# Products by halves around two norms, the first heads' groups turned beside the last items, half-width sums of squares added up by GpSimd

## The reference, cut to what matters

```python
def trunk_layer(x, mod, lw, lam, l_init, ffn, ctx):
    shift1, scale1, gate1, shift2, scale2, gate2 = jnp.split(mod, 6, axis=-1)
    h = rmsnorm(x, lw['norm_mix']) * (1 + scale1) + shift1
    y, state = token_mixer(h, lw, lam, l_init, ctx)      # 6 differential heads | convolution | 6 latent heads, then @ w_out
    x = x + gate1 * y
    h = rmsnorm(x, lw['norm_ffn']) * (1 + scale2) + shift2
    x = x + gate2 * ffn(h)                               # layer 0: dense SwiGLU; layer 1: top 2 of 8 experts
    return x, state

def rmsnorm(x, g):
    xf = x.astype(F32)
    y = xf * lax.rsqrt(jnp.mean(xf * xf, axis=-1, keepdims=True) + EPS)
    return (y * g.astype(F32)).astype(x.dtype)
```

## Time and profile before

| what | value |
|---|---|
| time, median of 3 runs | 2053.76 us (2052.38 to 2057.56) |
| span of the profiled execution | 2053.3 us; the page gives no other time for it |
| PE busy | 1881.8 us, 92% |
| DVE busy | 1393.7 us, 68% |
| ACT busy | 1022.6 us, 50% |
| POOL busy | 311.6 us, 15% |
| PE's share of the chain that ended last | 77% |

### The profile page before, as it was taken

One profiled execution on the slowest core, in us unless ns is written; L12 is line 12 of the kernel. 1 busy time (PEld: TensorE's weight loads), 2 busy tenths in 40 slices (PEclk: granted clock), 3 DMA queues, 4 the chain that ended last, 5 costly groups with the idle time before them and its releaser, 6 DMA issues.

```text
span 2053.3 us, 28528 instructions
## 1 busy us (share of the span) xinstructions
PE 1881.8 (92%) x11244; PEld 1701.7 (83%) x11244; DVE 1393.7 (68%) x1956; ACT 1022.6 (50%) x1371; POOL 311.6 (15%) x491
## 2 busy tenths in 40 slices
PE   5999789897999999997998789897999999999994
PEld 3987678697999999997988678696788888888883
DVE  5375885535666567555474885535898988898987
ACT  4235686623221211213135686623777777777772
POOL 0082540000000000000073541010000000000002
PEclk8999799998999999998999799997999999999998
DMA  9225300022454444422122000014999999999996
GB/s 330 63 92 194 99 1 1 21 89 96 134 164 155 134 159 144 139 83 67 53 68 71 1 1 1 1 23 156 399 391 405 404 407 389 404 399 395 375 396 230
DMA packets 112438, 366.22 MB, mean 178 GB/s; under 512 B 7456, under 2 KB 65216, under 8 KB 85936
## 3 DMA queue, kind: packets, MB, share of 16 engines
q1 hardware_dynamic: 94448, 303.50, 39.3%
q0 software_dynamic: 13536, 48.39, 7.1%
q10 hardware_dynamic: 4320, 12.49, 1.5%
HBM read 349.23 MB, written 15.12 MB: 177 GB/s over the span
## 4 chain that ended last, share of the span: by engine, by line
PE 77%; DVE 11%; ACT 5%; DMA 3%; issue 3%; POOL 1%; SPq 0%; DVEq 0%; POOLq 0%; ACTq 0%
PE PS L2108 33%; PE PS L2049 25%; PE PS L2088 5%; PE PS L1777 5%; PE PS L1893 4%; PE PS L1865 3%; ACT E L844 2%; DVE NM L1217 1%; ACT PT L849 1%; DVE KCn L1177 1%; DMA araw<-in_w_ada_head 1%; DVE E L1228 1%; DVE SS L1160 1%; DVE split L1497 1%; DMA raw<-in_w_ada_head 1%
## 5 line engine op out<-in xcount | busy, mean ns | idle before, releaser
L2108 PE MATMUL PS<-H,split 128*128 128x320 f32 x2688 | 402.9, 312 | 8.8 <-DVE H L1697 7.2
L2108 PEld LDWEIGHTS PS<-H,split 128*128 128x128 f32 x2688 | 400.8, 191 | 11.9 <-issue 10.8
L1019 ACT CAST split<-raw 128x2048 fp32r<-128x2048 f32 (+2 forms) x64 | 112.8, 1763 | 284.3 <-PE PS L2108 242.1
L1497 DVE TENSOR_TENSOR split<-raw,split 128x2048 fp32r<-128x2048 f32 (+2 forms) x64 | 138.0, 2161 | 126.5 <-ACT split L1019 126.5
L1412 DVE TENSOR_TENSOR msplit<-raw,msplit 128x2048 fp32r<-128x2048 f32 x82 | 187.9, 2292 | 37.0 <-ACT msplit L976 37.0
L2049 PE MATMUL PS<-split,HT 128*128 128x512 f32 x816 | 197.0, 397 | 2.8 <-DVE HT L1391 2.4
L1412 DVE TENSOR_TENSOR split<-raw,split 128x2048 fp32r<-128x2048 f32 x82 | 186.8, 2289 | 18.3 <-ACT split L976 18.3
L976 ACT CAST msplit<-raw 128x2048 fp32r<-128x2048 f32 x82 | 157.0, 1915 | 70.4 <-PE PS L2049 61.6
L2049 PE MATMUL PS<-msplit,HT 128*128 128x512 f32 x816 | 191.0, 389 | 0.7 <-DVE msplit L1412 0.7
L1777 PE MATMUL PS<-split,H 128*128 128x384 f32 (+1 forms) x960 | 171.1, 340 | 12.8 <-DVE split L1497 9.5
L2049 PEld LDWEIGHTS PS<-split,HT 128*128 128x128 f32 x816 | 152.8, 191 | 34.5 <-DVE HT L1391 2.8
(11 more groups left out here) (326 smaller groups left out, 2827.1 us busy)
## 6 DMA issues: line engine op xcount, KB each, us to landing
raw<-in_moe_w_gate SPq DMA_DIRECT2D x55, 1024.0 KB, 7.5
raw<-in_moe_w_down SPq DMA_DIRECT2D x55, 1024.0 KB, 7.9
raw<-in_moe_w_up SPq DMA_DIRECT2D x54, 1024.0 KB, 7.3
DOTW<-in_w_ada_rows POOLq DMA_DIRECT2D x56, 512.0 KB, 3.9
raw<-in_w_ada_head SPq DMA_DIRECT2D x16, 1024.0 KB, 7.1
mraw<-in_moe_w_up SPq DMA_DIRECT2D x14, 1024.0 KB, 7.2
mraw<-in_moe_w_gate SPq DMA_DIRECT2D x13, 1024.0 KB, 7.3
mraw<-in_moe_w_down SPq DMA_DIRECT2D x13, 1024.0 KB, 7.8
```

Source lines behind the costliest of these rows:

```text
L1019: A.copy(split[u % 2][:, 0, 0:w], src[:, 0:w]).then_inc(S["split_hi"], 1)
L1497: V.tensor_tensor(split[u % 2][:, 1, 0:w], src[:, 0:w], split[u % 2][:, 0, 0:w].bitcast(f32), ALU.subtract).then_inc(S["split_lo"], 1)
L2108: ins = T.matmul(PS[:, 4 * (u % 2) + 2 * c + hf, 0:HALF], W[:, w, k, c * P:(c + 1) * P], A[:, a, k, hf * HALF:(hf + 1) * HALF], start=(k = ...
```

## The change

Four things. (1) The two units before and the two units after norms 1 and 2 run as *pairs* by halves of 320 tokens: first half of both units, then second half of both. The norm runs on the first half of the tokens while PE does the second half of the pair ahead of it, and on the second half while PE does the first half of the pair behind it. The reciprocal root is copied from PSUM to `RSTD` in SBUF by ACT, and sums and roots are taken for three groups of columns per half. (2) For chunks 4 to 7 the squares are 320 wide, in `SQH`, and GpSimd adds them to `XACC`. (3) The five `QA` groups are turned in iterations 53 to 57, through bank 1, and the convolution's high part is rounded in iteration 58; after the last item only the `OC` groups are left, and the first output unit starts on the `QA` chunks when four of them are turned, the fifth being turned behind its first chunk. (4) PE's loop over the FFN rounds is written out. Buffers are moved (`H`, `MIX`, `QA`, `KA`, `VA`, `VC`, `KCn`, `ACTB`) so that the halves don't overwrite what is still read.

```diff
+K_MIX = ITEMS - NT - 2
@@ GpSimd
+            def add_half_squares(q):
+                first = SQUARES[q] + 4
+                for i in range(8):
+                    hf = i // 4
+                    pool.wait_ge(S["sq_ready"], first + i + 1)
+                    pool.wait_ge(S["sq_used"], first + i)
+                    acc = XACC[:, hf * HALF:(hf + 1) * HALF]
+                    nc.gpsimd.tensor_tensor(acc, acc, SQH[:, i % 2, :], ALU.add).then_inc(S["sq_used"], 1)
@@ ScalarE, norm_halves (ua is the first unit of the pair ahead of the norm)
+                half_square(0, 4)
+                half_square(0, 5)
+                A.activation(XWARM[:, :], eps[:, :], ACT.Sqrt)
+                half_square(0, 6)
+                half_square(0, 7)
+                half_root(0)
+                rstd_copy(0)
+                split_hi(ua + 2)
+                shifted_hi(0)
+                half_square(1, 4)
+                half_square(1, 5)
+                shifted_hi(1)
+                shifted_hi(2)
+                half_square(1, 6)
+                half_square(1, 7)
+                split_hi(ua + 3)
+                for i in range(3, 7):
+                    shifted_hi(i)
+                half_root(1)
+                shifted_hi(7)
+                rstd_copy(1)
+                for i in range(KC, 2 * KC):
+                    shifted_hi(i)
@@ VectorE, norm_halves
+                half_add(0, 0)
+                half_add(1, 0)
+                x_mean(q, 0)
+                x_rstd(q, 0)
+                half_add(0, 1)
+                scaled(0)
+                scaled(1)
+                split_lo(ua + 2)
+                shifted_lo(0)
+                scaled(2)
+                shifted_lo(1)
+                half_add(1, 1)
+                scaled(3)
+                shifted_lo(2)
+                for i in range(4, 7):
+                    scaled(i)
+                    shifted_lo(i - 1)
+                x_mean(q, 1)
+                scaled(7)
+                shifted_lo(6)
+                x_rstd(q, 1)
+                shifted_lo(7)
+                split_lo(ua + 3)
+                scaled(8)
+                for i in range(9, 2 * KC):
+                    scaled(i)
+                    shifted_lo(i - 1)
+                shifted_lo(2 * KC - 1)
@@ TensorE
             for k in range(-2, ITEMS + 1):
+                if 0 <= k - K_MIX < NT:
+                    t = k - K_MIX
+                    if t == 0:
+                        pe.wait_ge(S["turn_out"], (l + 1) * TURNS)
+                    else:
+                        pe.wait_ge(S["mix_lo"], l * 10 + t)
+                    pe.wait_ge(S["subln_gained"], l * NT + t + 1)
+                    mix_turn(t, 1, QA[:, t, :])
                 if k + 2 < ITEMS:
...
-            for w in range(2 * NT):
...
-            pe.wait_ge(S["mix_lo"], (l + 1) * 10)
-            pe.wait_ge(S["conv_lo"], l + 1)
+            for i in range(4):
+                mix_turn(NT + i, 4 + i, OC[:, TILE_ORDER[i], :])
+            def mixed(k):
+                if k == 0:
+                    pe.wait_ge(S["mix_lo"], l * 10 + NT)
+                if k == 1:
+                    pe.wait_ge(S["mix_lo"], l * 10 + NT + 1)
+                    mix_turn(2 * NT - 1, 4, OC[:, TILE_ORDER[4], :])
+                if k == MIX_CONV[0]:
+                    pe.wait_ge(S["conv_lo"], l + 1)
+                if k == MIX_C[0]:
+                    pe.wait_ge(S["mix_lo"], (l + 1) * 10)
+            def first_half_sums(hf, i, k):
+                if (hf, i, k) == (1, 0, 4):
+                    x_sum_half(1, 0)
+                if (hf, i, k) == (1, 1, 0):
+                    x_rows_half(1, 0)
...
+            def pair(u, k_chunks, A, ready=None, free=None, halves=False):
+                for hf in range(2):
+                    for i in range(2):
+                        v = u + i
+                        if hf == 0:
+                            free(v)
+                            pe.wait_ge(S["split_lo"], v + 1)
+                        W = split[v % 2][:, :, 0:k_chunks * 256].rearrange("p s (k n) -> p s k n", k=k_chunks)
+                        for k in range(k_chunks):
+                            if ready is not None:
+                                ready(hf, i, k)
+                            for c in range(2):
+                                for w, a in ((0, 0), (0, 1), (1, 0)):
+                                    ins = T.matmul(PS[:, 4 * (v % 2) + 2 * c + hf, 0:HALF], W[:, w, k, c * P:(c + 1) * P],
+                                                   A(a, k, hf),
+                                                   start=(k == 0 and w == 0 and a == 0), stop=(k == k_chunks - 1 and w == 1))
+                        if hf:
+                            ins.then_inc(S["unit_used"], 1)
+                        elif halves:
+                            ins.then_inc(S["half_used"], 1)
...
+                    def h_half(hf, i, k, q=q):
+                        if (hf, i, k) == (0, 0, 5):
+                            x_sum_half(q, 1)
+                        if (hf, i, k) == (0, 1, 0):
+                            x_rows_half(q, 1)
+                        if i == k == 0:
+                            pe.wait_ge(S["rstd_copied"], 2 * (q - 1) + hf + 1)
+                        if i == 0:
+                            pe.wait_ge(S["h_lo"], NORMED_H[q] + hf * KC + k + 1)
-            with pe.Fori(0, rounds) as r:
-                round_(r, u0, 4, KC, r * 4)
-            round_(None, u0 + rounds * ROUND, tail, TAIL_FF // P, rounds * 4)
+            for r in range(rounds):
+                round_(u0 + r * ROUND, 4, KC, r * 4, first=r == 0)
+            round_(u0 + rounds * ROUND, tail, TAIL_FF // P, rounds * 4, last=True)
```

More of the change, by code:

```diff
@@ L871, in mixer_act @@
                     unit_squares(2 * l + 1, k - 2, base + U_OUT + k - 2)
-                if l == 1 and k == 4:
+                if k == 4:
                     act.wait_ge(S["tables_ready"], 4)
@@ L882, in round_ @@
                 d_pairs, d_u = extra
-                for k in range(2 * pairs + 4):
+                for k in range(2 * pairs + (2 if last else 4)):
                     if k < 2 * pairs:
@@ L899, in round_ @@
                         unit_squares(2 * l + 2, k - 2 * pairs, u0 + k)
+                if last:
+                    norm_halves(2 * l + 2, u0 + 2 * pairs + 2)
             u0 = base + U_FFN
@@ L1204, in invert, with mix_lo @@
                     ch.then(ins)
+            def mix_lo(w, bank, chunks, t):
+                dve.wait_ge(S["mix_hi"], l * 10 + w + 1)
+                V.tensor_tensor(MIX[:, mix_slots(l, 1, chunks), t * P:(t + 1) * P],
+                                PS[:, bank, 0:3 * P].rearrange("p (c n) -> p c n", c=3),
+                                MIX[:, mix_slots(l, 0, chunks), t * P:(t + 1) * P].bitcast(f32), ALU.subtract).then_inc(
+                    S["mix_lo"], 1)
             for k in range(-2, ITEMS + 1):
@@ L1447, in round_ @@
                 n_units = 2 * pairs + 4
-                for k in range(n_units):
+                for k in range(n_units - 2 if last else n_units):
                     if k < 2 * pairs:
@@ L2059, in moe_pe, with ffn_pe, unit_free, first_half_sums @@
                 piece(n)
-        def ffn_pe(T, pe, l, base, turn, product, h_ready):
+        def ffn_pe(T, pe, l, base, product, pair, h_half, x_sum_half, x_rows_half):
             rounds, tail = layer_rounds(l)
-            acts0 = 0
-            def round_(r, u0, pairs, kd, d_pairs):
+            def unit_free(u):
+                pe.wait_ge(set_free[u % 2], products_before(u, u % 2))
+            def first_half_sums(hf, i, k):
+                if (hf, i, k) == (1, 0, 3):
+                    x_sum_half(2, 0)
+                if (hf, i, k) == (1, 1, 1):
+                    x_rows_half(2, 0)
+            def round_(u0, pairs, kd, d_pairs, first=False, last=False):
@@ L2076, in round_ @@
-                    product(u, KC if k < 2 * pairs else kd, H if k < 2 * pairs else ACTB, r, ready)
-            u0 = base + U_FFN
-            with pe.Fori(0, rounds) as r:
-                round_(r, u0, 4, KC, r * 4)
-            round_(None, u0 + rounds * ROUND, tail, TAIL_FF // P, rounds * 4)
+                    if first and k < 2:
+                        if k == 0:
+                            pair(u, KC, halves_of(HH[1]), ready=h_half, free=unit_free)
+                        continue
+                    if last and k == 2 * pairs + 2:
+                        pair(u, kd, halves_of(ACTB), ready=first_half_sums, free=unit_free, halves=True)
+                        break
@@ L2095, in x_sum, with x_sum_half @@
                 ins.then_inc(S["x_summed"], 1)
-            def product(u, k_chunks, A, r=None, ready=None):
-                pe.wait_ge(S["split_lo"], u + 1 + (0 if r is None else r * ROUND))
+            def x_sum_half(q, hf):
+                pe.wait_ge(S["sq_used"], SQUARES[q] + 8 + 4 * hf)
+                for i, first in enumerate(half_tiles(hf)):
```

(5 more changed lines are left out.)

394 lines of the change are left out of this document (253 added, 141 removed).

## The result

| | before | changed |
|---|---|---|
| time, median | 2053.3 us, 4 runs (2052.38 to 2057.56) | 2027.89 us, 4 runs (2027.52 to 2031.09) |
| span of the profiled execution | 2053.3 us | 2025.8 us |
| ratio, 95% interval | 1 | 0.9855 (0.982 to 0.989) |
| ratio in a second measurement (e9) | 1 | 0.9889 (0.9861 to 0.9918) |

By these ratios the change makes the kernel 1.1 to 1.5% faster (the medians alone give 1.2 and 1.0%); 1.0% was forecast, just outside the first interval and inside the second. Between the two profiles lie 27.5 us, where 21.0 were forecast. The kernel before, run again beside the experiments, took from 2050.92 to 2067.13 us in 34 executions, a spread of over half the gain, so what follows compares stretches of the profiles and not only times.

What follows compares the result with a forecast made beforehand. PE was taken as the bound, carrying 77% of the chain. Norms 10.9, turned groups 8.5 and loop 1.6 made 21.0 us off the 2053.3 span: 2032.3, so a median of 2033 us, range 2024 to 2045.

Steps and rivals of the forecast that it cites:

- The norms: Norms 1 and 2 run by halves of the tokens: gains of 7.2 and 3.7 us, together 10.9.
- the second half's pace: Second unit's first half starts 16.4 us (norm 1) and 19.1 (norm 2) behind the last half unit ahead, paced by DVE.
- the exclusion: At the norms, GpSimd's adds and DVE's two-input instructions exclude one another; norm 1's loss 10.9 us, without it 9.0.
- the chain without adds: DVE's steps at each norm without GpSimd's adds: second unit's half 14.5 and 17.2 us behind the last unit ahead.
- the clock: PE's clock may drop in the half-idle first half unit behind each norm: 0.5 us a norm, 3.5 as other bound.
- The turned groups: End of each layer's items: five groups turned among the items, first output unit earlier; 4.25 us gained a layer, 8.5 together.
- the stretch of the items: Last item iterations of a layer: PE's turns wait for DVE's `mix_lo`, making the stretch 2.9 us longer net.
- The loop: PE's loop over the FFN rounds, written out: saves its boundary of 1.57 us in the chain, once.
- rival A: Halves hide the norms nearly whole, GpSimd blocks nobody, clock stays up: 29.5 us gained, 2024 us; chance 0.12.
- B: Slower pair pace from long handovers and low clock, items swallow the turned groups' gain: 2045 us; chance 0.21 with D.
- C: Half units themselves dearer, three matmuls adding into one bank: 21 us more at 176 ns a matmul; chance 0.05.
- D: At the norms a late `split` holds PE as long as before: 2044 us; chance 0.21 together with B.

Runs made afterwards that it cites:

- e9: The changed kernel run again, the same program, against the kernel before; 2032.6 us, ratio 0.9889 (0.9861 to 0.9918).
- e3: The changed kernel with GpSimd's eight adds a norm cut to one column; 2030.24 us in one run.
- e2: The changed kernel with the first heads' five groups turned behind the last item again, norms still by halves; 2027.09 us in one run.
- e8: The kernel of e2 with the first output unit also waiting for all ten groups' and the convolution's low parts before its first product; 2041.68 us in one run.

## Why the prediction was right or wrong

**The norms: direction right, and the second half's pace, the step that failed, too dear by 4.0 us in all.** Forecast 7.2 and 3.7, measured 9.4 and 5.5. The second unit's half was to start at T + 16.4 and T + 19.1; it starts at T + 14.6 and T + 17.5. Its terms, one by one:

First, the exclusion: "Four adds of 0.85 fall between T-3 and T+5.6, among DVE's chunks", charged with 1.9 at both norms on top of the wait "ahead of chunk 3" for ACT's rounding. The exclusion is real (e3: 0.68 against 1.3). The Trainium skill's rule in GPSIMD Engine Reference, Specifications, that the two contend when DVE reads two inputs out of SBUF, is borne out, and so is the row that I took it from the earlier trace rows; that `half_add` would be spared no run shows, since no add falls beside it. But the last two adds were over by T + 3.4, and the stretch and the wait for ACT cover one another: without the adds DVE waits 1.08 for ACT, with them not at all. What counts of the 2.4 of stretch is some 0.7 at norm 1 and 1.3 at norm 2 (an estimate from e3's waits).

Second, the chain without adds, which I gave as T + 14.5 and 17.2. e3 has 14.2, with 0.8 of low clock in it, and 15.3. At norm 1 DVE had chunk 1 done at T + 0.5 and not T + 1.5, and the second half's addition 1.1 earlier for it; of the 1.8 between forecast and measurement the other 0.7 lies between that addition and chunk 3. Which of my step lengths ahead of T made the 1.1 I did not follow up.

Third, the clock. The 0.5 a norm was of the right size, and not hidden behind DVE: 0.7 at norm 1 in the changed kernel, none there in e9, about 1.0 at norm 2. That the second norm is "2.7 later" came out (2.9) by luck: without the adds it is 1.1, in e9 3.6, since clock and exclusion are not the same at the two norms.

**The turned groups: the sum right, its cause wrong.** Forecast 4.25 a layer, measured 4.5 and 4.6; the stretch of the items forecast as 2.9, measured 2.7, and its wait where it was said to be. But I put the gain down to turning five groups early. e2 shows that this is worth nothing on balance: 2.7 lost among the items, 2.3 to 3.0 won behind them. The gain is in one line of the diff that I worked out as a small term ("DVE has the last group's low part by 410, needed at 415"): the unit now waits for each part at the chunk that needs it (e8). The sum has a slip too: of the 1.9 that the unit loses to the low clock "I keep half" would be 0.95, and I added 0.1. The unit did gain 0.6 (15.25 instead of 15.88, with 0.35 of turns in it), and it started 2.65 behind the last result where I had 1.8, so the two errors cancel. A sum can be right with wrong entries, and only undoing one part at a time shows it.

**The loop: 1.57 forecast, 1.6 to 1.8 measured.**

**What was not in the sum.** Stretches with the same code differ by 1.8 us between the two profiles, net; A alone by 2.3. That is below the 6 us that I called indistinguishable, and with the 4.7 us of the terms above it makes the 27.5.

**The rivals.** By its number the result, 2027.9, lies between rival A (2024) and the forecast (2033), nearer to A, and at the norms the 14.9 gained is nearly A's 15.9. A's mechanism did not come all the same: GpSimd does stretch DVE, the clock does not stay up, and the norms still cost 9.2 and 12.8; its number was nearly met because the rest of the chain is shorter than I had it. B did not come, since the exclusion was milder than in its long handovers (the bounds have slips: 8.8 and 6 are 14.8, so the lower one is -4 and not -3, and without exclusion and clock loss norm 2 gains 18.4 - 12.3 = 6.1, not 6.3). C, dearer half units, is refuted: the three half units from 477.06 to 498.25 are 144 matmuls at 147 ns, the pace of whole units. D is refuted by columns D and E of the table.

## What to carry to other kernels

Before moving work ahead of a long operation, look at what that operation waits for: letting it start on the part of its input that is there may give all of the gain, and the move none on top of it (here 4 to 5 us a layer). A second engine that adds for a busy VectorE out of the same SBUF is not free; count its adds as VectorE's own, then ask which wait the stretch lies over: two delays that cover one another are charged once. When a change is worth 1%, compare the stretches that it touches, cut at events, and not only the total.

## What the runs showed of the hardware

**The clock's falls move between executions, and move the time with them.** Its code is the same in all kernels but for where buffers lie, and A came out at 155 to 158 us in nine of the profiles of the table and at 162 to 163 in five. A few other stretches show it too, as B1 of e8 (27.25, and 22.83 in the other kernels that turn no groups there). The windows of before, of the changed kernel and of e9, its repetition, show where it begins:

```profile
248.00:252.00 4.00, 3.82 (x19) 3.83 (x20) 2.94 (x7) 2.38 (x6) 2.57 (x3) 0.51 0.02 4
252.00:256.00 4.00, 4.00 (x25) 4.00 (x24) 1.81 (x6) 2.08 (x7) 0.34 (x1) 0.64 0.00 0
```

```profile
244.00:248.00 4.00, 2.72 (x12) 2.73 (x13) 3.25 (x9) 3.20 (x8) 1.72 (x3) 0.57 0.00 0
248.00:252.00 4.00, 3.88 (x36) 3.69 (x35) 3.71 (x9) 3.38 (x10) 2.91 (x4) 1.00 0.02 4
```

```profile
248.00:252.00 4.00, 3.49 (x18) 3.27 (x17) 2.94 (x5) 2.93 (x7) 2.56 (x3) 0.60 0.02 4
252.00:256.00 4.00, 4.00 (x22) 4.00 (x21) 2.07 (x7) 2.00 (x6) 0.34 (x1) 0.50 0.00 0
```

The changed kernel and e9 are one program. In the one the granted clock is low in the first of these windows and back in the second; in the other it falls a window later and stays low through the third. By ACT's exponentials e9 is 3.9 us behind the changed kernel after this stretch, and before, whose fall is shorter, 2.3. e9 loses another 2.9 at 368 to 376 us, where its clock falls again and the changed kernel's does not (changed, then e9):

```profile
368.00:372.00 4.00, 4.00 (x28) 3.23 (x27) 2.58 (x7) 2.04 (x6) 1.67 (x2) 1.00 0.00 0
368.00:372.00 4.00, 4.00 (x22) 3.84 (x21) 1.98 (x9) 1.52 (x4) 1.00 (x1) 0.53 0.00 0
```

The five profiles with A at 162 to 163 are the five that have this second fall, and the same five have the long first one. Together that is up to 7 us in A alone, more than one norm's gain. What decides between the two courses was not found.

**GpSimd suffers as much as VectorE**: an add of 320 columns takes 872 ns at the median and 1977 at most, beside a split of 2048 columns that itself kept its 2.29.
